# A hybrid DeltaNet / Conformer layer on one core: latent keys of head pair 0 projected with the context keys' weights

## What is computed

```python
mod   = silu(c) @ w_mod + b_mod            # 2048 x 12288: shift, scale, gate (twice); mod_c from c_ctx
h     = rms_norm(x)   * (1 + scale) + shift          # latent tokens
hc    = rms_norm(ctx) * (1 + scale_c) + shift_c      # context tokens
p, pc = h @ w_in, hc @ w_in[:, :STATE_END]           # q, k, v (8 heads of 128), beta/g, z, conformer a and gate
q, k, v = silu(depthwise_conv5(.)), l2 norm of q and k        # of either sequence
state_c       = bidir_gated_delta(kc, vc, beta_c, g_c, 0)     # context: only the final states are kept
o             = bidir_gated_delta(q, k, v, beta, g, state_c)  # latent: starts from them
mix   = [rms_norm(o) * silu(z), conformer_branch(a, gate)]
x     = x + gate1 * rms_norm(mix @ w_out)
x     = x + gate2 * rms_norm(swiglu(modulated rms_norm(x)) @ w_down)
```

## Time and profile before

| | |
|---|---|
| three runs | 1611.95, 1611.73, 1609.91 us |
| the profiled execution | 1613.92 us |
| its span, first to last instruction | 1612.2 us |
| TensorE (PE) busy | 1538.3 us |
| VectorE (DVE) busy | 1033.4 us |
| ScalarE (ACT) busy | 739.2 us |
| GpSimd (POOL) busy | 222.2 us |
| moved by DMA | 334.58 MB |

### The profile page before, as it was taken

How to read it: one execution, slowest core, us unless ns; L and a number is a source line. 1 busy time by engine, 2 the same in 40 slices (tenths; PEclk the granted TensorE clock), 3 DMA queues, 4 the chain that set the end, 5 groups by cost and what they waited for, 6 DMA issues and landing times.

```text
span 1612.2 us, 25110 instructions
## 1 busy us (share of the span) xinstructions
PE 1538.3 (95%) x9297; PEld 1295.0 (80%) x9297; DVE 1033.4 (64%) x1435; ACT 739.2 (46%) x1042; POOL 222.2 (14%) x236
## 2 busy tenths in 40 slices
PE   3888999999999999999999999999999999999998
PEld 0557888898889888898877888888888888888786
DVE  1446899999997766665577544545454454777554
ACT  5535534443345745455357444444444443443332
POOL 2000223333242324244100000000000000000000
PEclk9998999999999999999999999999999999999999
DMA  9994566555655556564373766666666666998653
GB/s 351 382 397 116 167 199 196 190 190 183 208 179 176 171 171 209 170 196 132 118 261 117 212 194 186 192 185 192 184 193 192 187 190 191 339 321 319 222 187 136
DMA packets 190977, 334.58 MB, mean 208 GB/s; under 512 B 14706, under 2 KB 80354, under 8 KB 189985
## 3 DMA queue, kind: packets, MB, share of 16 engines
q1 hardware_dynamic: 190194, 330.89, 63.3%
q0 software_dynamic: 688, 2.39, 0.5%
HBM read 331.15 MB, written 2.10 MB: 207 GB/s over the span
## 4 chain that ended last, share of the span: by engine, by line
PE 82%; DVE 9%; DMA 2%; ACT 2%; SPq 2%; issue 2%; DVEq 0%; ACTq 0%
PE PS L1886 67%; DVE cacc L1752 3%; DMA first<-in_w_mod_dram 2%; DVE w_lo L1465 2%; PE PS L2107 2%; PE PS L2155 2%; PE PS L1892 2%; PE PS L2201 2%; SPq L756 2%; DVE sil L1586 1%; PE PS L2053 1%; PE PS L2097 1%; PE PS L1982 1%; DVE xyi L1645 1%; ACT L973 1%
## 5 line engine op out<-in xcount | busy, mean ns | idle before, releaser
L977 ACT ACTIVATE w_hi<-raw 128x1024 fp32r<-128x1024 f32 (+1 forms) x422 | 443.2, 1056 | 494.8 <-PE PS L1886 418.1
L1432 DVE TENSOR_TENSOR w_lo<-raw,w_hi 128x1024 fp32r<-128x1024 f32 x264 | 323.0, 1225 | 309.9 <-ACT w_hi L977 309.8
L1886 PE MATMUL PS<-w_hi,h_hi 128*128 128x512 f32 x704 | 275.2, 391 | 0.0
L1886 PE MATMUL PS<-w_hi,h_lo 128*128 128x512 f32 x704 | 274.3, 390 | 0.0
L1886 PE MATMUL PS<-w_lo,h_hi 128*128 128x512 f32 x704 | 274.1, 389 | 0.0
L1886 PE MATMUL PS<-h_hi,w_hi 128*128 128x256 f32 (+1 forms) x784 | 237.6, 303 | 0.0
L1465 DVE TENSOR_TENSOR w_lo<-raw,w_hi 128x1024 fp32r<-128x1024 f32 (+1 forms) x158 | 195.8, 1250 | 56.5 <-ACT w_hi L977 56.5
L1886 PE MATMUL PS<-h_hi,w_lo 128*128 128x256 f32 (+1 forms) x784 | 221.5, 283 | 0.0
L1886 PE MATMUL PS<-h_lo,w_hi 128*128 128x256 f32 (+1 forms) x784 | 221.4, 282 | 0.0
L1886 PEld LDWEIGHTS PS<-h_hi,w_hi 128*128 128x128 f32 (+1 forms) x784 | 148.3, 189 | 36.1 <-issue 32.0
L1886 PEld LDWEIGHTS PS<-w_hi,h_lo 128*128 128x128 f32 x704 | 132.3, 188 | 27.6
(11 more groups left out here) (323 smaller groups left out, 2338.4 us busy)
## 6 DMA issues: line engine op xcount, KB each, us to landing
raw<-in_w_in_dram SPq DMA_DIRECT2D x128, 512.0 KB, 3.8
raw<-in_w_mod_dram SPq DMA_DIRECT2D x96, 512.0 KB, 5.3
raw<-in_w_gate_dram SPq DMA_DIRECT2D x88, 512.0 KB, 3.6
raw<-in_w_up_dram SPq DMA_DIRECT2D x88, 512.0 KB, 3.6
raw<-in_w_down_dram SPq DMA_DIRECT2D x88, 512.0 KB, 4.6
first<-in_w_mod_dram SPq DMA_DIRECT2D x64, 512.0 KB, 9.3
raw<-in_w_out_dram SPq DMA_DIRECT2D x32, 512.0 KB, 4.3
gin<-in_w_mod_dram SPq DMA_DIRECT2D x32, 512.0 KB, 6.0
```

What stands on the lines that cost most here:

```text
L977: act.activation(out_ap, in_ap, ACT.Copy).then_inc(S[kind], 1)
L1432: dve.tensor_tensor(w_lo[:, slot, :], raw[:, (R0 + n) % RING, :], w_hi[:, slot, :].bitcast(F32), ALU.subtract).then_inc(S["lo"], 1)
L1886: ins = pe.matmul(out_ap, a[i], b[j], start=start and n == 0, stop=stop and n == 2, skip_group_check=grouped)
```

## The change

- The latent keys of pair 0 move from the 17th place of `STREAM` to the second, so into `EARLY`; the context values of pair 0 move from the second to the fifth, with all four units behind the startup. Some latent groups behind that change places.
- The four units of the context keys of pair 0 become shared units `("both", "k", g)` of eight parts: one load and one split; parts 0 to 3 for the context, 4 to 7 for the latent tokens. `SPREAD` becomes (2, 4, 5, 6), and all split steps of the latent tokens of a quarter stand behind the first of its units.
- The steps that take the two early key groups out of PSUM get slots of their own (`"early"`); the second tap step of the group beside `ba` is no longer put ahead of `ba`.
- The natural latent keys of pair 0 are kept in the tile `sctx` of context pair 3 until they are normalised (`natural`); the state steps of context pair 3 are placed behind that, the normalising behind the last state step of context pair 2. Other steps get such placement rules too.
- All numbers of `AFTER` are new; `ba` of the latent tokens stands beside the group at place 5 instead of 4.

```diff
-SPREAD = (2, 3, 5, 6)
+SPREAD = (2, 4, 5, 6)
...
-STREAM = [("k", CTX, 0), ("v", CTX, 0), ("g", LAT, 0), ("a", LAT, 0), ("k", CTX, 1), ...
+STREAM = [("k", CTX, 0), ("k", LAT, 0), ("g", LAT, 0), ("a", LAT, 0), ("v", CTX, 0), ("k", CTX, 1), ...
...
-MIX = {"ba0": 1, "ba1": 4}
+MIX = {"ba0": 1, "ba1": 5}
...
-              ([("xf", old[0]), ("nx", old[1])], [(AFTER["xf"][m - 1], ("nx", old[0]))]), ([("xf", old[1])], [(AFTER["xf1"][m - 1], ("nx", old[1]))])]
+              ([("xf", old[0]), ("nx", old[1])], [(AFTER["xf"][m - 1], ("nx", old[0]))] + (
+                  [(0, ("vn", (*PAIRS[m - 2], 1)))] if m > 1 else [])), ([("xf", old[1])], [(AFTER["xf1"][m - 1], ("nx", old[1]))])]
...
-            ([("kn", (s, "k", p))], [(AFTER["kn"][m], ("nsq", (s, "k", p)))]),
+            ([("kn", (s, "k", p))], [(AFTER["kn"][m], ("nsq", (s, "k", p)))] + ([(0, ("st", (CTX, 2, 1)))] if m == NP else [])),
...
-            ([("mneg", k) for k in both], [(AFTER["mneg"][m], ("mlo", old))] if m else []),
+            ([("mneg", k) for k in both], [(AFTER["mneg"][m], ("mlo", old))] if m else [(0, ("nbe", (CTX,)))]),
...
+    held = {(CTX, NP - 1): [(0, ("kn", (LAT, "k", 0)))], (LAT, 0): [(0, ("mix_lo", (NP + 3,)))]}.get((s, p), [])
...
-            ch.append(([("st", (s, p, i)), ("stc", (s, p, i))], [(AFTER["st"][m], ("vn", (s, p, i)))]))
+            ch.append(([("st", (s, p, i)), ("stc", (s, p, i))], [(AFTER["st"][m], ("vn", (s, p, i)))] + held))
...
+    if cu in EARLY and what == "k":
+        at = AFTER["early"][EARLY.index(cu)]
+        return [], [(at[0], [("tap2", cu), ("tapa", cu)]), (at[1], [("taps", cu)]), (at[2], [("csilu", cu)]),
+                    (at[3], [("nat", cu), ("natc", cu)])], []
...
+    def early_unit(cu, g):
+        if cu[0] != "k":
+            unit(("win", cu, g), QS, beside)
+            return
+        u = ("both", "k", g)
+        if cu[1] == CTX:
+            plan.extend([("hi", (u,)), ("lo", (u,))])
+        products(u, range(QS * cu[1], QS * cu[1] + QS), beside)
...
-            cu, g = early.pop(0)
-            unit(("win", cu, g), QS, beside)
-            plan.extend(lat[:3])
-            del lat[:3]
+            early_unit(*early.pop(0))
+            plan.extend(lat)
+            del lat[:]
...
-            if cu[0] in "kvq":
+            if cu[0] in "kvq" and cu not in EARLY:
                 put([("taps", cu)])
...
+            if u[0] == "both":
+                col = CU_COL[u[1]]
+                return w_in_v[:, 4 * u[2]:4 * u[2] + 4, col:col + 256]
...
+        def natural(what, m):
+
+            if m == NP and what == "k":
+                return sctx[:, NP - 1, :, :].rearrange("p a b -> p (a b)").rearrange("p (t h d) -> p t h d", t=NT, h=2)
+            return kvq[what][:, m % 2, :, :, :]
...
-                    elif u[0] == "win":
+                    elif u[0] in ("win", "both"):
                         cu, g = u[1:]
+                        if u[0] == "both":
+                            cu = (u[1], part // QS, 0)
+                        part = part % QS
```

More of the change, by code:

```diff
@@ L89 @@
 GAP = {"solve": 2, "state": 4, "ready": 2}
[L90 removed]
[5 rows of a table removed]
[L96 to L100, removed]
[L103 removed]
+AFTER = {"nr": [4, 7, 4, 7, 3, 4, 2, 3], "nr_last": [2, 18, 6, 13, 5, 5, 0, 7], "nx": [0, 0, 0, 0, 0, 0, 0, 0],
[5 rows of a table added]
+         0, 2, 0, 1], "mneg": [4, 7, 4, 2, 5, 6, 0, 10], "kc": [10, 8, 8, 11, 8, 8, 1, 3], "mhi": [3, 0, 13, 3, 7, 0, 5, 4],
+         "qnsq": [0, 9, 2, 0, 2, 0, 14, 0], "qn": [0, 2, 0, 0, 0, 0, 0, 0], "qT": [0, 4, 2, 15, 4, 5, 4, 4], "qfree": [0, 12,
+         2, 0, 6, 0, 1, 0], "qk": [0, 0, 0, 0, 0, 0, 0, 0], "qT2": [7, 0, 11, 10, 3, 3, 6, 6], "qk1": [3, 5, 0, 4, 0, 1, 0,
+         4], "taps": [0, 3, 5, 0, 1, 4, 5, 8], "csilu": [0, 6, 9, 10, 8, 8, 12, 12], "nat": [15, 13, 11, 0, 11, 13, 3, 8],
+         "gates": 18, "conv": 4, "rush": 1, "early": [[0, 1, 4, 5], [0, 4, 6, 15]], "vb1": [0, 0, 1, 0, 0, 0, 0, 3]}
+MIX = {"ba0": 1, "ba1": 5}
 def solved(m):
@@ L222, in unit, with products @@
         plan.extend([("hi", (u,)), ("lo", (u,))])
-        for part in range(parts):
+        products(u, range(parts), beside)
+    def products(u, parts, beside):
+        for part in parts:
             plan.append(("mm", (u, part)))
@@ L265, in follow @@
             m = PAIRS.index(key[1:]) if kind == "nat" else 0
-            if kind == "nat" and m >= (2 if key[0] in "kv" else NP + 2):
+            if kind == "nat" and key not in EARLY and m >= (2 if key[0] in "kv" else NP + 2):
                 s, p = PAIRS[m - 2]
@@ L323, in make_plan @@
         slot[2] = slot[0] + 16 * (rest.index("a") + 1 if "a" in rest else 4)
-        if cu == EARLY[-1]:
-            pass
-        for g in range(NQ - 1 if cu in EARLY else 0, 4):
-            unit(("win", cu, g), QS, beside)
-            done += cu not in EARLY
-            gates(MR * KT * done // total - (MR * KT - len(mr)))
+        if cu in EARLY:
+            early_unit(cu, NQ - 1)
             plan.extend(lat)
             del lat[:]
+        else:
+            for g in range(4):
+                unit(("win", cu, g), QS, beside)
+                done += 1
+                if True:
+                    gates(MR * KT * done // total - (MR * KT - len(mr)))
         now, then, later = evacuation(cu)
         put(now)
-        soon += [(slot[0] + wait, steps) for wait, steps in then]
+        last = soon[-1][0] if soon and cu not in EARLY else 0
+        for wait, steps in then:
+            last = max(last, slot[0] + wait)
+            soon.append((last, steps))
+        soon.sort(key=lambda x: x[0])
         late += later
@@ L653, in layer @@
                 projected.append(u if u[0] == "ba" else u[1])
+        projected = EARLY + [w for w in projected if w not in EARLY]
         proj_bank = {w: n if n < len(EARLY) else (n - len(EARLY)) % 2 for n, w in enumerate(projected)}
@@ L659, in layer @@
         held = {proj_bank[w]: w for w in EARLY}
-        last_unit = {w: (w, 0) if w[0] == "ba" else (("win", w, 3), QS - 1) for w in projected}
+        last_unit = {w: (w, 0) if w[0] == "ba" else (
+            ("both", w[0], 3), QS * w[1] + QS - 1) if w in EARLY[:2] else (("win", w, 3), QS - 1) for w in projected}
         conv_cus = [cu for cu in CUS if cu[0] in "kvq"]
@@ L1149, in _ @@
                     k = PAIRS.index((s, p))
-                    if k >= 2:
+                    if k >= 2 and key not in EARLY:
                         before = PAIRS[k - 2]
@@ L1159, in _ @@
                         need(act, "vn", CTX, 2, 1)
-                    copy(kvq[what][:, k % 2, :, :, :].rearrange("p t h d -> p (t h d)"),
+                    copy(natural(what, k).rearrange("p t h d -> p (t h d)"),
                          PS[:, BANK["nat", key], :], kind)
@@ L1227, in _ @@
                         tile, h = divmod(n, 2)
-                        ins = act.activation(gmv[:, tile, h, :], kvq[what][:, m % 2, tile, h, :], ACT.Square,
+                        ins = act.activation(gmv[:, tile, h, :], natural(what, m)[:, tile, h, :], ACT.Square,
                                              accum_out=sums[:, a + n:a + n + 1])
@@ L1594, in _ @@
                     a = 8 if what == "k" else 12
-                    kq = kvq[what][:, PAIRS.index((s, p)) % 2, :, :, :].rearrange("p t h d -> p (t h) d")
-                    dve.tensor_tensor(kq, kq, bc(rstd[:, a:a + 4], 2, P), ALU.mult).then_inc(done, 1)
+                    m = PAIRS.index((s, p))
+                    if m == NP and what == "k":
+                        need(dve, "kd", CTX, 2, 1)
+                    kq = kvq[what][:, m % 2, :, :, :].rearrange("p t h d -> p (t h) d")
+                    dve.tensor_tensor(kq, natural(what, m).rearrange("p t h d -> p (t h) d"), bc(rstd[:, a:a + 4], 2, P), ALU.mult).then_inc(done, 1)
                 elif kind == "gk":
```

10 lines of the change are left out of this document (6 added, 4 removed), and 10 rows, old and new, of the table AFTER.

## The result

Seven runs of the kernel after took 1615.85 to 1620.39 us, median 1618.29 us; seven of the kernel before on the same chip 1609.91 to 1614.1 us, median 1611.95 us. The ratio is 1.0041 (95% interval 1.0031 to 1.005): **slower by 6.3 us**, where the forecast had it faster by 6.0. The profiled execution took 1615.85 us (span 1614.1), the fastest of its seven, while the one of before (1613.92) is among the slower of its own. So the two profiles differ by 1.9 us where the medians differ by 6.3, and one more execution of each is among the experiments.

The account below looks back on a forecast made before the run. TensorE bounds the kernel (busy 1538.3 of 1612.2 us), with DMA full early and DVE also at its limit from 200 to 500 us. Gains 3.3 + 1.2 + 1.5 = 6.0 us from 1611.7 give 1605.7 us; range 1599.5 to 1613.

Parts of the forecast that it names:

- Loads: Startup: three weight loads fewer end the modulation products 2.6 to 3.9 us earlier; 3.3 us taken as gain.
- The tail sum: Startup's end: from step 28 no slack, four steps and three units, 13.1 us, so modulation ends at 119.3 to 120.6.
- the startup gives nothing: Rival, chance 0.18: gate load or PE eats the startup gain, 3.3 falls to 1 or less; 1609 to 1611 us.
- Gate load: Startup: small gate load ahead of the last modulation weights costs nothing, 0.4 us of cover; 1.1 us if cover is gone.
- Gate projection's wait: After the startup: PE's wait for the context keys' last tap step falls 1.2 us to 2.1; bounds 0 and 2.5.
- Splits removed: Startup and 200 to 500 us: fewer splits, groups pushed back 16 parts, an eighth of PE's waits saved, 1.5 us.
- Distances: Solve, state and output chain: latent keys ready long before, queue behind gets some 13 parts of slack; value left to a rival.
- slack, priced as a rival: Rival, chance 0.22: 13 parts of slack cut chain waits by a third and one half clock, 5.4 us for 1.5; 1601.8 us.
- The bounds of one new stall against half the waits: Range of the splits term, 200 to 500 us and chain waits: loss of one 3.9 us stall, or gain of 6.
- The rival "slower": Chance 0.13: three more low splits on full DVE, 200 to 500 us, make steps late; two stalls give +3.3, 1615.0 us.

Follow-up runs that it names:

- 4: Kernel before, context values of pair 0 multiplied with the shared key weights (four loads and split pairs fewer), order and distances kept: 1609.23 us, ratio 0.998.
- 14: Kernel before, context values of pair 0 multiplied with the shared key weights, and SPREAD (2, 4, 5, 6): 1608.79 us, ratio 0.9985.
- experiment 16: Kernel after with the first pair's seed one part later (2 to 3), 390 steps moved: 1646.46 us, ratio 1.0206.
- experiment 11: Kernel before with the first pair's seed one part later (2 to 3), 245 steps moved: 1628.88 us, ratio 1.0104.
- 6: Kernel after with three distances raised by three or four (first seed, kT and nx of context pair 3): 1653.03 us, ratio 1.0256.
- 2: Kernel after with the old AFTER distances of the kernel before, only the entry `early` kept new: 1657.78 us, ratio 1.0285.
- 7: Kernel before with about half the depthwise convolution taps left out: 1599.1 us, ratio 0.9922.
- 8: Kernel after with about half the depthwise convolution taps left out: 1605.45 us, ratio 0.9962.
- 1: Kernel after with the latent keys' scale and tap steps of pair 0 put ahead of the gate unit: 1618.99 us, ratio 1.0045.

## Why the prediction was wrong

**Loads (forecast -3.3 us).** Right in kind: nine loads, an earlier end of the startup, and less waiting for DMA between 40 and 125 us in the mean (4.9 us over the 13 traces with nine loads, 6.7 over the 5 with twelve; not the 2 that I named, and the second execution of after has 6.5). In size it was half: 1.5 us in the mean. The tail sum rested on one execution of before, and its 122.14 us was the latest of five; this term had no row for how far it varies. The rival "the startup gives nothing", with 1 or less for this term, was nearer than the forecast, and the whole saving with the order kept measured 2.7 and 3.1 us by the medians (experiments 4 and 14).

**Gate load (0).** No sign of a cost: in the eleven traces of kernels with the order of after the last modulation product came at 121.6 us at the latest, before's latest is 122.1, and `SPREAD` made no difference.

**Gate projection's wait (forecast -1.2, to 2.1 us).** Right in kind: the two tap steps follow each other, and in the three kernels with the order of after in the table above the wait is 1.96, 3.11 and 1.96 us, mean 2.3, against 3.31, 3.56 and 3.08 in three of before. The wait also depends on when PE arrives, as experiments 4 and 14 show: their tap steps follow each other too, and the wait is 4.42 and 3.03 us. From mark 1 to the gate's first product it is 16.6 us in the mean of the three of before, 15.8 in the three of after, and 15.6 in experiments 4 and 14. So 0.8 to 1.0 us of the 1.2 came. I kept the half clock behind it; this is what came, with the wait at 151 us beside it (kernel after, table in steps of 1 us):

```profile
136.00:137.00 1.00, 1.00 (x11) 0.94 (x9) 0.00 (x0) 0.99 (x2) 0.00 (x0) 1.00 0.05 16
...
152.00:153.00 1.00, 1.00 (x7) 1.00 (x6) 1.00 (x2) 1.00 (x2) 0.00 (x0) 0.50 0.03 8
```

Behind 1.96 us of idling the granted clock stayed at 1.00 (2.4 GHz); behind 2.99 us it was 0.50 (1.2 GHz), 7 instructions in a microsecond in place of 11.

**Splits removed (forecast -1.5, bounds +4 and -6) and Distances (slack, priced as a rival).** Here the forecast failed. These two steps took the order and the table of numbers as one thing with room in it: groups move by 16 parts, the chain has 13 parts of slack, DVE gets a little relief, so PE's waits fall by an eighth. The mixer became 5.9 us longer where gate and splits together were to make it 2.7 shorter. Three things in these steps were wrong.
First, the slack is not there to be spent. By the plan's counting the last context solve ends at part 290 in the kernel after, 277 before, and the first latent one starts 17 parts behind it in place of 27: the reorder had used the room itself. In experiment 16 the shift runs on into the latent pairs, up to part 453. And where there was room it did not help: in experiment 11 no step behind part 318 moves, and one part's shift cost 17 us, against 27 in 16 and 35 for four parts (6). My reading is that the chain is held by what stands next to each step on an engine, not by how late its last step is; that is argued, not shown.
Second, a reorder makes the old numbers worthless and must buy them back: +46 us unfitted, +6 fitted (2). I gave the refit no cost, because the step costed only what the diff removes. The bounds of one new stall against half the waits had no row behind them that bore on this.
Third, relief of DVE does not pay here. DVE lost 11.5 us of work between 200 and 300 us and PE gained nothing, and halving the convolution leaves the difference at 6.35 us (7, 8).
I also overlooked the bank of the context values, 2.99 us of wait; that turned out to cost nothing by itself (1).

**The rival "slower"** had the sign, the stretch and, with 1615.0 us, half of the amount (3.3 of 6.3). Its mechanism, three more low splits on a full DVE, is not borne out: the loss stays when DVE is at 80%. Its form, a few new stalls of 2.5 to 3.3 us with half clock behind some, is what the trace shows (151.06, 380.89, 460.85). PE's idle time from 200 to 500 us rose from 11.2 to 15.6 us, by 4.4; the forecast had named a change of over 4 as what would refute it. (Over three traces of each order it is 11.2 to 11.5 and 13.8 to 16.1 us, 3.7 apart in the mean.)

**Where the loss sits, in sum.** In the three traces of each kind in the table above, PE idles 28.1 and 30.7 us in the mean between 123 and 763 us, and the half clock costs 6.9 and 8.9 us (busy time times what the granted clock lacks of 1.00, over windows of 1 us). That is 4.6 of the 5.9 us; about another one is the wait behind the last modulation product, 2.8 us in both, of which up to 2 us lie before 123 us, and so are not counted, where the startup ends earlier.

**What stays open.** No run shows that the new order has no better table: none of my few edits of it made it faster, which is no search. That order, rules and table together cost about 9 us against the saving with the order kept is shown; why they fit worse is only argued, by the latent keys' taps, which now stand near part 60 in place of 274, ahead of the first solve, by their normalising at part 276 in place of 290, and by most convolution chunks, which come 16 parts later. No kernel here that computes the whole layer beats the one before; experiments 4 and 14 show that some 3 us are to be had if the key weights could be shared without moving the groups.

## What to carry to other kernels

In engines that walk one list in order, a table of hand-placed distances is part of the order: price a reorder at the refit, and first shift one number by one to see how sharp the fit is. Three stalls taken out or shortened alone gave nothing here, and other waits came in their place, so count the waits over the whole stage and not one by one. And a term that rests on one traced execution needs the spread of that mark over two or three.

## What was not expected of the hardware

A convolution chunk on DVE has one length alone and another beside GpSimd. Timeline of DVE and of GpSimd (POOL), kernel after:

```profile
270.56 1.50 DVE L1791 SCALAR_TENSOR_TENSOR cacc<-ub,vcol,cacc 128x212 f32<-128x212 f32 x4
275.98 2.61 DVE L1791 SCALAR_TENSOR_TENSOR cacc<-ub,vcol,cacc 128x220 f32<-128x220 f32 x4
...
276.32 1.30 POOL L955 TENSOR_TENSOR mkl<-kc,lvl 128x512 fp32r<-128x512 f32 x1 [7.84 <-PE PS L2139]
```

Four instructions take 1.50 us alone and 2.61 us beside one GpSimd operation of 1.30 us, that is, 1.1 us longer; at 376.53, beside two GpSimd operations of 3.05 us together, 3.70 us. The tap steps, whose first operand is in PSUM, don't lengthen: eight took 3.98 us at 131.17 with GpSimd idle and 3.97 at 146.84 beside two of its operations of 0.61 us, and four took 2.02 us at 174.18 beside one of 1.28. The Trainium skill (SBUF — State Buffer, SBUF: two separate sides) says that the two engines share one port pair: of a VectorE instruction with two SBUF inputs and a GpSimd instruction that reads SBUF, the one that starts first holds it for its whole length, and the other waits. The rows agree. The same lengthening is in the kernel before. Summed over DVE's instructions from 123 us on (length beside GpSimd less the median length of the same kind with GpSimd idle), it is 38.0 to 39.9 us in three traces of before's order and 38.8 to 39.3 in three of after's, so its sum does not explain the loss. But it makes a DVE instruction's length depend on what stands beside it, and so a chunk moved by one part can be 2 us longer ahead of a step that PE wants; the wait at 380.89 is such a case. That this is why the tables are so sharp is not shown; no run here isolates it.
